# One modulation vector moved from TensorE to VectorE in the first layer's input projection

## What is computed

```python
def modulation(cond, w_mod, b_mod):
    m = jax.nn.silu(cond) @ w_mod + b_mod          # (2048) @ (2048, 6*2048)
    return jnp.split(m[..., None, :], N_MOD, axis=-1)
...
    sm, cm, gm, sf, cf, gf = modulation(c, mod_w[l], mod_b[l])
    h = rms_norm(xs, norm_mix_pre[l]) * (1 + cm) + sm
    q_a, k_a, v_a, q_b, k_b, v_b, u_c, v_c = split_projection(h, w_in[l])   # h @ w_in, 4608 columns
    ...
    xs = xs + gm * rms_norm(merge_heads(o_a, o_b, o_c, w_out[l]), norm_mix_post[l])
    xs = ffn_sublayer(xs, sf, cf, gf, norm_ffn_pre[l], norm_ffn_post[l], w_gate[l], w_up[l], w_down[l])
```

## Time and profile before

| what | value |
|---|---|
| median of 3 runs | 2339.31 us (2339.07 to 2342.21) |
| profiled execution: time | 2339.66 us |
| profiled execution: span | 2337.9 us |
| mean granted TensorE clock | 0.991 |
| TensorE matmul / VectorE / ScalarE busy | 97% / 69% / 42% |
| start stage, first to last `w_in` matmul | 38.15 to 295.7 us |

### The profile page before, as it was taken

One profiled execution on the slowest core, in us unless ns is written; L12 is line 12 of the kernel. 1 busy time (PEld: TensorE's weight loads), 2 busy tenths in 40 slices (PEclk: granted clock), 3 DMA queues, 4 the chain that ended last, 5 costly groups with the idle time before them and its releaser, 6 DMA issues.

```text
span 2337.9 us, 27817 instructions
## 1 busy us (share of the span) xinstructions
PE 2256.9 (97%) x10614; PEld 1783.4 (76%) x10614; DVE 1623.0 (69%) x1734; ACT 985.3 (42%) x1277; POOL 66.0 (3%) x96
## 2 busy tenths in 40 slices
PE   5999979999999999999999998899999999999998
PEld 3666656678888888888877886687888888888886
DVE  3555464489988889989887996557888544555455
ACT  3333243464444444334446344347444444433443
POOL 1000120000000000000000101000000000000000
PEclk9999999999999999999999999999999999999999
DMA  9899979868878878888866997766887666666664
GB/s 352 324 344 333 348 257 346 285 223 293 287 265 293 287 266 285 285 278 290 308 207 223 313 314 237 282 196 208 258 276 264 193 190 189 190 189 196 191 221 149
DMA packets 269285, 609.91 MB, mean 261 GB/s; under 512 B 19084, under 2 KB 19264, under 8 KB 267808
## 3 DMA queue, kind: packets, MB, share of 16 engines
q1 hardware_dynamic: 264832, 589.37, 75.1%
q0 software_dynamic: 4320, 18.75, 2.2%
HBM read 603.79 MB, written 5.45 MB: 261 GB/s over the span
## 4 chain that ended last, share of the span: by engine, by line
PE 86%; DMA 6%; DVE 4%; ACT 2%; issue 1%; POOL 1%; SPq 1%; POOLq 0%; DVEq 0%; ACTq 0%
PE bank_A L870 41%; PE bank_B L870 38%; DMA mraw<-in_mod_w 5%; PE bank_M L929 2%; PE bank_X L954 2%; DVE wlo L1469 1%; PE bank_M L918 1%; ACT junk L1190 1%; ACT whi L1176 0%; DVE acc L1490 0%; DMA x<-in_x_sample 0%; DVE x L1579 0%; SPq L575 0%; PE bank_M L859 0%; PE bank_A L1054 0%
## 5 line engine op out<-in xcount | busy, mean ns | idle before, releaser
L1469 DVE TENSOR_TENSOR wlo<-raw,whi 128x1024 fp32r<-128x1024 f32 x724 | 880.2, 1222 | 589.6 <-ACT whi L1176 588.9
L1176 ACT CAST whi<-raw 128x1024 fp32r<-128x1024 f32 x724 | 759.4, 1051 | 1164.9 <-PE bank_A L870 578.0
L870 PE MATMUL bank_B<-whi,xt_lo 128*128 128x512 f32 x1104 | 433.3, 392 | 0.0
L870 PE MATMUL bank_A<-whi,xt_lo 128*128 128x512 f32 x1088 | 429.1, 394 | 3.7 <-DVE xt_lo L1520 3.7
L870 PE MATMUL bank_B<-wlo,xt_hi 128*128 128x512 f32 x1104 | 429.9, 389 | 0.0
L870 PE MATMUL bank_B<-whi,xt_hi 128*128 128x512 f32 x1104 | 429.8, 389 | 0.0
L870 PE MATMUL bank_A<-wlo,xt_hi 128*128 128x512 f32 x1088 | 425.1, 391 | 0.0
L870 PE MATMUL bank_A<-whi,xt_hi 128*128 128x512 f32 x1088 | 424.9, 390 | 0.0
L1490 DVE SCALAR_TENSOR_TENSOR acc<-mraw,cond,acc 128x1024 f32<-128x1024 f32 x300 | 371.2, 1279 | 0.0
L870 PEld LDWEIGHTS bank_A<-whi,xt_lo 128*128 128x128 f32 x1088 | 205.1, 189 | 64.5 <-issue 22.3
L870 PEld LDWEIGHTS bank_B<-whi,xt_lo 128*128 128x128 f32 x1104 | 207.2, 188 | 53.9 <-issue 10.9
(11 more groups left out here) (232 smaller groups left out, 1571.1 us busy)
## 6 DMA issues: line engine op xcount, KB each, us to landing
mraw<-in_mod_w SPq DMA_DIRECT2D x372, 512.0 KB, 5.9
raw<-in_w_gate SPq DMA_DIRECT2D x176, 512.0 KB, 4.4
raw<-in_w_up SPq DMA_DIRECT2D x176, 512.0 KB, 4.5
raw<-in_w_down SPq DMA_DIRECT2D x176, 512.0 KB, 5.0
raw<-in_w_in SPq DMA_DIRECT2D x144, 512.0 KB, 5.5
raw<-in_w_out SPq DMA_DIRECT2D x64, 512.0 KB, 5.8
z<-in_mod_w SPq DMA_DIRECT2D x8, 512.0 KB, 13.8
gate_mix<-gate_rows POOLq DMA_DIRECT2D x4, 1024.0 KB, 8.6
```

Of the source, the lines that this page charges most:

```text
L870: mm = pe.matmul(bank[f"{pair}{s}"][:], xs[:, k, t], w[:, kb, :], start=(k == first and n == 0), stop=(k == (nk - 1 if last is None else l ...
L1176: act.copy(weights(u * UNIT + ph)[0], raw[:, ph % RING]).then_inc(hi_ready, 1)
L1469: dve.tensor_tensor(lo, raw[:, ph % RING], hi.bitcast(F32), ALU.subtract).then_inc(lo_ready, 1)
```

## The change

Vector 2 goes from `MOD_PE` to the front of `MOD_DVE`. Its 32 pieces are accumulated by VectorE behind the splits of pieces 3 to 64 (`FIRST_FROM`, `FIRST_TO`), nearly every second one. They don't use the ring `mraw`: `first_piece` loads them into three places of their own, `hid`, `sil` and `cv` (`cv` is moved in SBUF for it), behind the raw load two pieces ahead of the piece of their accumulation. The first three wait until TensorE is done with all of the first 16 modulation pieces (`mod_used`), later ones for the accumulation three before. The accumulators are `qkt` and the first half of `f`. TensorE loses the 8 bursts of vector 2 and gets the reduction behind piece 64; the 12 bursts of vectors 0 and 1 now stand at 1, 4, 7, 10 of each of the first three quarters, and the first of vector 3 stays at 67. In quarter 0 ScalarE reads the banks into `z` (`read_first`) instead of VectorE. GpSimd's attention loads wait for the reduction instead of piece 62.

The diff, without the declaration of the three semaphores `vector_landed`, a wait for `ones_ready` that moves to the first reduction, and its lines of context:

```diff
 MOD_INIT = 2 * ND
-MOD_WIN = W_INC // 2
+MOD_WIN = 0
...
     return g - RING if g - RING not in EXTRA else g - 2 * RING
-MOD_PE = [2, 3, 4, 10]
-MOD_DVE = [5, 6, 7, 8, 9, 11]
+MOD_PE = [3, 4, 10]
+MOD_DVE = [2, 5, 6, 7, 8, 9, 11]
+FIRST_DVE = 2
+RING_DVE = MOD_DVE[1:]
+FIRST_FROM, FIRST_TO = 3, 64
+FIRST_PLACES = 3
...
 def dve_piece_at(v, i):
+    if v == FIRST_DVE:
+        return FIRST_FROM + (FIRST_TO - FIRST_FROM) * i // (MPIECES - 1)
...
-    return FFN_PIECE[0] + 7 + DVE_SPAN * (MPIECES * MOD_DVE.index(v) + i) // (4 * MPIECES - 1)
+    return FFN_PIECE[0] + 7 + DVE_SPAN * (MPIECES * RING_DVE.index(v) + i) // (4 * MPIECES - 1)
...
 DVE_PIECES = {dve_piece_at(v, i): (v, i) for v in MOD_DVE for i in range(MPIECES)}
-MOD_FETCH = {g - 3: e for g, e in DVE_PIECES.items()}
+MOD_FETCH = {g - (2 if v == FIRST_DVE else 3): (v, i) for g, (v, i) in DVE_PIECES.items()}
...
     if v is None:
-        return m * UNIT + j + MPIECES * sum(d < vector_of(m) for d in MOD_DVE)
-    return MOD_INIT * UNIT + MPIECES * (v - 2) + i
+        return m * UNIT + j + MPIECES * sum(d < vector_of(m) for d in RING_DVE)
+    return MOD_INIT * UNIT + MPIECES * (v - FIRST_DVE - 1) + i
...
     return n, r // 2, 2 * n + r % 2
-START_BURSTS = [QUARTER * n + r for n, rs in enumerate(((1, 4, 7, 10, 14), (1, 4, 7, 10, 13, 16), (1, 4, 7, 10, 13, 16), (1, 4, 7, 13)))
+START_BURSTS = [QUARTER * n + r for n, rs in enumerate(((1, 4, 7, 10), (1, 4, 7, 10), (1, 4, 7, 10), (13,)))
                 for r in rs]
 START_MOD = {g: (2 + i // 2, range(4 * (i % 2), 4 * (i % 2) + 4)) for i, g in enumerate(START_BURSTS)}
-START_ENDS = {g: m for g, (m, js) in START_MOD.items() if js[0] and (m < MOD_INIT or m == MOD_INIT + ND - 1)}
-ATT_PIECE = QUARTER * 3 + 8
+START_ENDS = {g: m for g, (m, js) in START_MOD.items() if js[0] and m < MOD_INIT}
...
         z = sb("z", [P, 2, W_IN])
+        cv = sb("cv", [P, NH + KVB, P])
         qkt = sb("qkt", [P, 20, P])
-        cv = sb("cv", [P, NH + KVB, P])
...
         def acc_of(v, h, s):
+            if v == FIRST_DVE:
+                return f[:, s, 0:KB * CH] if h else qkt[:, 8 * s:8 * s + 8, :].rearrange("p h c -> p (h c)")
...
             return t.rearrange("p (t n) -> p t n", t=KB)
+        def first_place(i):
+            return (hid[:], sil[:], cv[:, 0:8, :])[i % FIRST_PLACES].rearrange("p t n -> p (t n)")
...
                     return
-                for v in MOD_DVE:
+                for v in RING_DVE:
...
-                sp.wait_ge(mod_used, q - MPIECES * sum(ring_piece(v=v) <= q for v in MOD_DVE) + 1)
+                sp.wait_ge(mod_used, q - MPIECES * sum(ring_piece(v=v) <= q for v in RING_DVE) + 1)
...
+            def first_piece(i):
+                h, k = divmod(i, KD)
+                if i < FIRST_PLACES:
+                    sp.wait_ge(mod_used, 2 * UNIT)
+                else:
+                    sp.wait_ge(acc_step, dve_op(FIRST_DVE, i - FIRST_PLACES, 1) + 1)
+                n = FIRST_DVE * D + h * KB * CH
+                sp.dma_start(first_place(i), a["mod_w"][0, k * P:(k + 1) * P, n:n + KB * CH]).then_inc(
+                    vector_landed[i % FIRST_PLACES], 16)
...
                     v, i = MOD_FETCH[u * UNIT + ph]
+                    if v == FIRST_DVE:
+                        return first_piece(i)
...
                 pool.wait_ge(xt_ready, xt_count(l, 0))
-                pool.wait_ge(w_used, (plan.at[(l, "win")][0] + 4) * UNIT if l else ATT_PIECE)
+                if l:
+                    pool.wait_ge(w_used, (plan.at[(l, "win")][0] + 4) * UNIT)
+                else:
+                    pool.wait_ge(acc_read, MOD_DVE.index(FIRST_DVE) + 1)
...
                         mod_tail(START_ENDS[q - 2])
+                    dve_vector(q)
...
                     split(0, q + LEAD)
+                    if n == 0 and r % 2:
+                        read_first(r // 2, q)
...
+            def read_first(c, q):
+                act.wait_ge(w_used, q + 1)
+                for s in range(2):
+                    b = f"{'AB'[c % 2]}{s}"
+                    act.copy(z[:, s, c * CH:(c + 1) * CH], bank[b][:]).then_inc(freed[b], 1)
...
                 h, k = divmod(i, KD)
-                q = ring_piece(v=v, i=i)
-                mraw_ready(dve, q)
-                w = mraw[:, q % RING].rearrange("p t n -> p (t n)")
+                if v == FIRST_DVE:
+                    dve.wait_ge(vector_landed[i % FIRST_PLACES], 16 * (i // FIRST_PLACES + 1))
+                    w = first_place(i)
+                else:
+                    q = ring_piece(v=v, i=i)
+                    mraw_ready(dve, q)
+                    w = mraw[:, q % RING].rearrange("p t n -> p (t n)")
...
                     split(0, q + LEAD)
-                    if r % 2:
+                    if n and r % 2:
...
                     t = z[:, s, c * CH:(c + 1) * CH]
-                    if n:
-                        dve.tensor_tensor(t, t, bank[b][:], ALU.add).then_inc(freed[b], 1)
-                    else:
-                        dve.tensor_scalar(t, bank[b][:], 1.0, None, ALU.mult).then_inc(freed[b], 1)
+                    dve.tensor_tensor(t, t, bank[b][:], ALU.add).then_inc(freed[b], 1)
...

```

More of the change, by code:

```diff
@@ L414, in build_program @@
         first_landed = [sem(f"first_landed_{i}") for i in range(2 * UNIT - RING)]
+        vector_landed = [sem(f"vector_landed_{i}") for i in range(FIRST_PLACES)]
         mod_used = sem("mod_used")
@@ L855, in dve_vector @@
                     v = MOD_REDUCE[g]
+                    if v == FIRST_DVE:
+                        pe.wait_ge(ones_ready, 1)
                     pe.wait_ge(acc_step, dve_op(v, MPIECES))
@@ L937, in mod_tail @@
                     return
-                if m == MOD_INIT + ND - 1:
-                    pe.wait_ge(ones_ready, 1)
                 vector_turn(mod_tail_of(m))
```

## The result

| | before | after |
|---|---|---|
| median of the runs | 2339.31 us (2339.07 to 2342.21, 3 runs) | 2350.56 us (2347.81 to 2354.23, 4 runs) |
| profiled execution, time / span | 2339.66 / 2337.9 us | 2349.97 / 2348.1 us |
| mean granted clock | 0.991 | 0.988 |

A fourth run of the kernel before took 5843.56 us and is left out of its median, which would be 2340.76 us with it. The ratio is 1.0042, 95% interval [1.0027, 1.0056]: the changed kernel is **slower, by 6 to 13 us**. The prediction said 2331 us and a range of 2322 to 2338.

A forecast was written before the change was run, and what follows sets the result against it. It took TensorE (97% busy, 86% of the chain) as the bound, DMA a close runner-up. TensorE -16.1, VectorE +1.5, DMA +5 and start +1 sum to -8.6 us: from 2339.66 to a median of 2331 us, range 2322 to 2338.

The forecast's parts named there:

- bursts gone, reduction added: TensorE, first layer's input projection: eight bursts go, -17.0 us; a reduction behind piece 64 comes, +2.1 us.
- waits of the nine other bursts: TensorE: bursts' 3.9 us of transfer waits go, except 2.62 at piece 67, which stays: -1.3 us.
- GpSimd's loads: Twelve attention loads, issued 21 us before the stage's end instead of 34, still land in time: nothing charged.
- ScalarE's reads: First quarter: 9 pairs of bank reads, 10.4 us on an engine with 44 us free, cost nothing.
- The DMA term: First three quarters: transfers 0.64 us too long per burst period, 7.7 us in 12; two thirds taken, 5 us (0 to 13).
- Rival C: DMA keeps the first three quarters as long as before, mean at or under 349 GB/s: 2335, up to 2338 us; 22%.
- VectorE's term: Quarters' ends: cover nearly used up, 3.7 us left; 0.5 us lost at each of three ends, 1.5 us (0 to 10).
- 6 us of lead: VectorE's splits end 2.2 us after the cast starts, TensorE comes 8.2 us later; about 5 us of lateness just fits.
- The start: SP's `raw` loads stop until 32.2 us, so the burst behind piece 1 waits: 1 us (0 to 4).
- Rival D: VectorE becomes the bound, its accumulations waiting for their own `mod_w` pieces, 1.5 us each: +10 us, 2349; 10%.
- the waits for `mraw`: Sign: in the stage, bursts of vectors 0 and 1 wait 4 us or more for their loads, up from 2.
- the later start of attention: Sign that the forecast is wrong: attention behind the stage begins later relative to the stage's last matmul; no size given.

The follow-up runs named there:

- before_loads_late: Kernel before, with only GpSimd's twelve attention loads issued four pieces later (behind piece 65 instead of 61): 2343.35 us, ratio 1.0016.
- before_act_reads: Kernel before, with only ScalarE instead of VectorE reading the first quarter's banks: 2339.29 us, ratio 0.9997.
- ring_ahead: Changed kernel, with the ring's loads issued before vector 2's load of the same step in SP's queue: 2342.51 us, ratio 1.0018.
- spread: Changed kernel, with the 12 bursts of vectors 0 and 1 spread over more of each quarter: 2341.81 us, ratio 1.0005.
- short_sums: Changed kernel, all vector 2 accumulations but the first pair cut to 8 columns of 1024, loads kept, outputs wrong: 2342.0 us, ratio 1.0006.
- combo: Changed kernel, with ring loads ahead of vector 2's, bursts spread over the quarters, and `w_out`'s first loads one step earlier: 2337.0 us, ratio 0.9983.
- late_first: Changed kernel, with `FIRST_FROM = 9` instead of 3, so vector 2 begins six pieces later: 2358.69 us, ratio 1.0082.
- small_loads: Changed kernel, vector 2's loads after the first three cut to 64 columns of 1024, accumulations full, outputs wrong: 2339.11 us, ratio 0.9997.
- wout_first: Changed kernel, with `w_out`'s first four loads issued one step earlier, ahead of the ring loads of attention's first burst: 2347.39 us, ratio 1.0025.
- both_small: Changed kernel, with vector 2's accumulations cut to 8 columns and its loads after the first three to 64: 2334.65 us, ratio 0.9977.

## Why the prediction was wrong, step by step

The predicted terms beside what the traces show, up to attention's first turn:

| term | predicted | measured | how |
|---|---|---|---|
| bursts gone, reduction added | -14.9 | -14.9 | by count; the reduction is 1.85 us in the chain, as a burst was |
| waits of the nine other bursts | -1.3 | -4.6 | 4.6 before, 0 after |
| VectorE | +1.5 (0 to 10) | +6.2 | two gaps of 3.1 us at quarters' ends, without the slower matmuls behind the second |
| DMA, without the first two bursts | +5 (0 to 13) | +11.9 | waits 0 before, 11.9 after |
| start: bursts behind pieces 1 and 4 | +1 (0 to 4) | +4.7 | 3.4 before, 8.1 after |
| GpSimd's loads | 0 | +5.3 | gap 4.5 to 9.8 |
| left over | | +2.5 | some 2 us are matmuls at the lower clock: 1.6 behind the second late bank read, 0.4 behind the burst at piece 4 |
| sum | -8.6 | +11.1 | |

**TensorE**'s count was right. That the fourth quarter came out as said (56.5 predicted, 55.9) is partly luck: the wait behind piece 67, which the prediction let stand at 2.62 us, went away, since GpSimd's loads had moved (before_loads_late), and the slower matmuls behind the late bank read took 1.6 us back. **ScalarE's reads** were rightly costed at nothing (before_act_reads).

**The DMA term failed in its form**, not by its rate. "One burst period now carries 10.9 us of transfers at 408 GB/s, 0.64 us too long, in 12 periods 7.7 us" had the rate right (400 to 409 GB/s in eight of the nine windows of 5 us from 115 to 160). It treated the transfers as one flow, and then took two thirds. What it left out is whose transfer is late. Vector 2's load was needed two pieces later and stood ahead of four ring loads that a burst waited for; ring_ahead turned this round and got back 7.5 us of waits with the same bytes. The discount of a third was a hope that the raw places carry a lead; in the window with 29 GB/s the engines had room and nothing to move, so no more lead was laid up there. The change also took away the bursts at r = 13 and 16, whose loads had filled that hole: spread, which only puts some back late in the quarter, shortened the second quarter by 7.3 us, some 4 of them burst waits. The text's "SP issues these pieces without a wait of their own in nearly all cases" was wrong as well (23 waits), but short_sums shows that this did no harm.

By the Trainium skill ("DMA: Bandwidth & Descriptors", section "Where 436 GB/s comes from") the HBM side, about 358 GB/s per core, is what binds a load from HBM. The traces do not agree: those nine windows stood at 400 to 409 GB/s but for one of 362, and combo held 380 over a quarter of 71.8 us. Rival C rested on such a cap on the mean; the mean after was at 333 to 348, as C says, but not because of a cap, since combo's first two quarters held 380 and 363.

**VectorE's term failed in its margin.** "6 us of lead" was counted from a split to its matmul. The wait came at the other product of VectorE: the bank. Two column blocks alternate between two pairs, so a pair must be read within one block, 5.44 us, and behind the 4 us `part` stood a split, 2.39 us of accumulation and another split ahead of the read. short_sums, with the sums gone, brings both waits down to 0.8 us. The text had all the numbers (its "about 5 us" of falling back is longer than the slack) and checked them against the wrong deadline. No single wait for `wlo` is among those of PE.

**The start** was just above its upper end, and its reason covers the smaller part. In late_first, where SP's start is as before, the burst behind piece 1 waits 1.6 us instead of 2.6, but the one behind piece 4 waits 7.3 instead of 5.5. In small_loads, where only vector 2's first three loads come in full, that second burst waits 2.0 us and the first still 2.9: what the second burst meets is mostly the bytes of vector 2's later loads.

**GpSimd's loads**, "nothing is charged", failed outright. The check was whether they land before their own first use; whom they delay was not asked. It is `w_out`'s first loads, whose splits stand before the last bank reads in VectorE's queue (before_loads_late, +3.7 us net with that part alone, in the kernel before). In the changed kernel itself the loads were not moved back, so its 5.3 us are the measured gap and not a tested price; wout_first gets 3.5 of them back by the order in SP's queue.

**The range** was too narrow by its own terms. The sum with all upper ends, -16.1 + 10 + 13 + 4, is +10.9 us, 2350: nearly the result. That is luck too in part, since the sum has nothing for GpSimd's loads and the lower clock, and more for VectorE than it cost. Three of the costs (DMA, start, GpSimd's loads) feed on the same two lacks, an in-order SP queue and DMA engines with no room, and came out high together; VectorE's does not, as small_loads leaves it as it was. Rival D, the slower one, gave 2349 but by another mechanism, a wait for vector 2's own pieces, which the trace does not show: VectorE lost nothing there. Of the signs listed, the waits for `mraw` (4 us or more) and the later start of attention were the right ones to look at; VectorE's busy time in the second quarter (55.2 us) and the length of the last quarter came as said; the DMA share near 1.0 did not (0.91 to 0.94).

## What to carry to other kernels

When an edit moves loads, place them in the queue by deadline, and ask of each who stands behind it and needs it sooner; a mean rate with room in it says nothing of ten pieces that ask for everything and eight that ask for nothing. Measure an engine's lead against every buffer that it must give back, not only against what it produces. Where several unsure costs draw on the same scarce thing, don't take the middle of each: their upper ends can come together. Removing work that stood in the quiet part of a period also removes its transfers from there, and may be worth less than its own length.

## What was not expected of the hardware

After the burst behind piece 4 had stood for 3.1 us and more on its loads, TensorE came back at a granted clock of 0.73 (after, below) and 0.60 (late_first, where it stood for 4.1 us), with the first matmul behind at 0.80 us instead of 0.39. These are means of 5 us, between the full level (2.4 GHz) and half of it. In the kernel before, with waits of 1.75 and 0.23 us in that burst, the clock stayed at 1.00. The waits of 2.9 us for a bank, with dense matmuls on both sides, went both ways: after the first in the changed kernel (178.18) it stayed at 1.00, after the second (245.60) it fell to 0.66. Over all runs there are ten such waits, and behind eight of them matmuls took 0.63 us.

```profile
60.00:65.00 5.00, 1.81 (x10) 0.33 (x8) 2.90 (x3) 1.04 (x1) 0.00 (x0) 0.93 1.04 407
65.00:70.00 5.00, 5.00 (x17) 2.75 (x14) 0.71 (x1) 0.00 (x0) 0.00 (x0) 0.73 1.05 408
...
245.00:250.00 5.00, 4.40 (x13) 3.59 (x14) 5.00 (x5) 0.00 (x0) 0.00 (x0) 0.66 0.87 285
```

Second, while GpSimd's loads were landing in the kernel after, the engines were busy (share 1.01) at only 256 GB/s. In the kernel before it was the same at 270 to 275 us, behind the same loads: share 0.99 at 267 GB/s, where 408 GB/s go with a full share at 115 to 120 us. So these loads cost more engine time than their bytes say:

```profile
290.00:295.00 5.00, 5.00 (x28) 3.74 (x21) 2.25 (x3) 0.00 (x0) 0.00 (x0) 1.00 1.01 256
```

Third, the runs of the kernel before spread more than the three shown ahead: 31 runs of one session lay between 2333.91 and 2346.52 us, and a difference of a few us between two single executions says nothing. The 95% interval was 0.15% to either side with four runs of the changed kernel and 0.1% with ten against 31.

Left open: why burst waits of 10.7 us remain in both_small; and whether loading attention's data early would save the gap, which was not tried since its places overlap `sil` and `f`.
